# Two looped expert jobs are written out beside the four first experts of a mixture-of-experts layer

## What is computed

```python
def swiglu(x, w_gu, w_down, width):
    h = x @ w_gu
    return (jax.nn.silu(h[..., :width]) * h[..., width:]) @ w_down

def moe_swiglu(x, w_router, w_gu, w_down):
    logits = jnp.einsum('btd,de->bte', x, w_router)
    top_val, top_idx = lax.top_k(logits, TOP_K)          # TOP_K = 2
    gate = ...                                           # softmax of the two, zero elsewhere
    out = jnp.zeros_like(x)
    for e in range(N_EXPERTS):                           # 8
        out = out + gate[..., e:e + 1] * swiglu(x, w_gu[e], w_down[e], D_EXPERT)   # 3584
    return out
```

## Time and profile before

| | |
|---|---|
| median of three runs | 1716.98 us |
| the profiled execution, and its span | 1711.11 us, 1709.4 us |
| mean granted clock of TensorE | 0.972 |
| first-jobs stage (743.6 to 1198.8): TensorE, VectorE, ScalarE busy | 401.6, 127.9, 107.8 us of 455.2 |
| the same: share of the DMA engines, rate | 1.03, 400 GB/s |
| a looped job (1322.1 to 1441.0): TensorE, VectorE, ScalarE busy | 118.9, 104.6, 88.5 us of 118.9 |
| the same: share of the DMA engines, rate | 1.00, 379 GB/s |

### The profile page before, as it was taken

How to read it: one execution, slowest core, us unless ns; L and a number is a source line. 1 busy time by engine, 2 the same in 40 slices (tenths; PEclk the granted TensorE clock), 3 DMA queues, 4 the chain that set the end, 5 groups by cost and what they waited for, 6 DMA issues and landing times.

```text
span 1709.4 us, 27459 instructions
## 1 busy us (share of the span) xinstructions
PE 1598.7 (94%) x10674; PEld 1213.7 (71%) x10674; DVE 998.5 (58%) x1233; ACT 750.8 (44%) x829; POOL 139.5 (8%) x247
## 2 busy tenths in 40 slices
PE   8999999999988999999899989786899999999897
PEld 6768999998866666854445535454688888888685
DVE  4668655456645554672223212231788888888797
ACT  4225543335343223252213212221677777777575
POOL 1231000000032450020000000000000000000300
PEclk9999999999999999999999999898999999999998
DMA  9969554444142350059999999999999999999992
GB/s 240 255 163 304 140 166 142 139 136 137 59 139 61 114 159 9 2 221 409 403 395 404 406 404 400 404 402 397 410 401 369 397 376 360 403 356 384 388 361 108
DMA packets 232252, 466.83 MB, mean 273 GB/s; under 512 B 25205, under 2 KB 121620, under 8 KB 232129
## 3 DMA queue, kind: packets, MB, share of 16 engines
q1 hardware_dynamic: 217246, 426.81, 68.7%
q0 software_dynamic: 11744, 31.62, 6.1%
q10 hardware_dynamic: 3155, 6.93, 1.2%
HBM read 445.78 MB, written 19.99 MB: 272 GB/s over the span
## 4 chain that ended last, share of the span: by engine, by line
PE 76%; DMA 8%; DVE 6%; ACT 4%; issue 3%; POOL 1%; ACTq 0%; SPq 0%; POOLq 0%; DVEq 0%
PE ps L2726 10%; PE ps L2882 8%; PE ps L2883 8%; PE ps L2884 8%; PE ps L2163 6%; PE ps L2165 6%; PE ps L2164 6%; DMA raw<-in_moe_w_gu 4%; PE ps L2719 3%; PE ps L2720 2%; PE ps L2721 2%; PE ps L2568 2%; DMA raw<-in_moe_w_down 2%; PE ps L2531 2%; PE ps L2607 2%
## 5 line engine op out<-in xcount | busy, mean ns | idle before, releaser
L2014 DVE TENSOR_TENSOR w_lo<-raw,w_hi 128x2048 fp32r<-128x2048 f32 x168 | 383.2, 2291 | 62.2 <-ACT w_hi L1302 61.0
L1302 ACT ACTIVATE w_hi<-raw 128x2048 fp32r<-128x2048 f32 x168 | 322.3, 1919 | 133.6 <-PE ps L2884 116.0
L2020 DVE TENSOR_TENSOR w_lo<-raw,w_hi 128x2048 fp32r<-128x2048 f32 x42 | 96.3, 2292 | 229.1 <-ACT w_hi L1309 228.2
L2163 PE MATMUL ps<-x_hi,w_hi 128*128 128x304 f32 x656 | 202.8, 309 | 2.8 <-DVE x_lo L1566 1.7
L2165 PE MATMUL ps<-x_lo,w_hi 128*128 128x304 f32 x656 | 198.0, 302 | 0.0
L2164 PE MATMUL ps<-x_hi,w_lo 128*128 128x304 f32 x656 | 197.1, 300 | 0.0
L2882 PE MATMUL ps<-w_hi,g_hi 128*128 128x512 f32 x448 | 177.9, 397 | 12.3 <-DVE w_lo L2014 12.1
L2883 PE MATMUL ps<-w_lo,g_hi 128*128 128x512 f32 x448 | 176.2, 393 | 0.0
L2884 PE MATMUL ps<-w_hi,g_lo 128*128 128x512 f32 x448 | 176.2, 393 | 0.0
L1437 DVE TENSOR_TENSOR w_lo<-raw,w_hi 128x2048 fp32r<-128x2048 f32 (+4 forms) x129 | 135.5, 1095 | 67.8 <-ACT w_hi L1044 67.6
L2726 PE MATMUL ps<-raw,g_s 128*32 128x128 f32 (+3 forms) x1920 | 161.3, 377 | 10.3 <-DMA raw<-in_moe_w_gu 10.3
(11 more groups left out here) (472 smaller groups left out, 2506.0 us busy)
## 6 DMA issues: line engine op xcount, KB each, us to landing
raw<-in_moe_w_gu SPq DMA_DIRECT2D x224, 1024.0 KB, 9.9
raw<-in_moe_w_down SPq DMA_DIRECT2D x112, 1024.0 KB, 9.0
raw<-in_ffn_w_gu SPq DMA_DIRECT2D x44, 512.0 KB, 5.2
raw<-in_conv_w_in SPq DMA_DIRECT2D x16, 512.0 KB, 8.4
raw<-in_ffn_w_down SPq DMA_DIRECT2D x16, 512.0 KB, 4.5
kvn<-in_cache_ckv POOLq DMA_DIRECT2D x64, 128.0 KB, 3.5
kvn<-in_cache_ckv SPq DMA_DIRECT2D x64, 128.0 KB, 2.7
rows_in<-zrow POOLq DMA_DIRECT2D x13, 512.0 KB, 10.4
```

The lines of the kernel that those rows point to most:

```text
L1302: nc.scalar.activation(w_hi[:, u % SPLIT], raw[:, u % RAW], ACT.Copy).then_inc(hi_done, 1)
L2014: V.tensor_tensor(w_lo[:, u % SPLIT], raw[:, u % RAW], w_hi[:, u % SPLIT].bitcast(F32), ALU.subtract).then_inc(lo_done, 1)
L2020: V.tensor_tensor(w_lo[:, n % F_SPLIT], first_raw(k), w_hi[:, n % F_SPLIT].bitcast(F32), ALU.subtract).then_inc(lo_done, 1)
L2163: nc.tensor.matmul(out, hi, xh, start=start, stop=False, skip_group_check=True)
```

## The change

The first two jobs of the loop, called E and F, move into the written-out stage, so that six jobs, 252 units, are run there and two are left in the loop. E and F run as H does, in seven half-width steps, without extra rows. H, E and F make one stream, C, A and B (in that order) the other, and a unit of one alternates with a unit of the other. The streams have PSUM banks of their own: gates and ups of the wide one in 0 and 2, the narrow one's in 3 and 6 (C in 3 alone), H's extra rows in 1 and their output in 6. A turn still follows on its step's last unit, except that a wide job's last turn comes after one narrow unit.

H's extra rows now come after the main product instead of before it. The buffers of E and F come free when the unit is split. The token rows of E, F and the first looped job are fetched to `xrow` 12 units into the wide job before, or early in the list, and turned in banks 0 and 2 between the two last down units of the wide job before. The 128-row outputs of H and E are copied and stored by ScalarE (`early_out`) right behind their last units; F's is stored as H's was, in the first looped job. The job table's count is lowered by two, and waits in the loop count from there.

```diff
-SMALL_AFTER = (2, 2, 1, 2, 2, 1, 2)
+EARLY_JOBS = 2
+STATIC = FIRST_JOBS + EARLY_JOBS
+SMALL_ORDER = "CAB"
+BIG = "HEF"
+BIG_STEPS = 2 * STEPS - 1
+def big_units():
+    seq = []
+    for i, x in enumerate(BIG):
+        for s in range(BIG_STEPS):
+            seq += [[("gate", x, s, part)] for part in range(2)]
+            if s:
+                seq += [[("down", x, s - 1, part)] for part in range(2)]
+            seq += [[("up", x, s, part)] for part in range(2)]
+            if s < BIG_STEPS - 1:
+                seq[-1].append(("turn", x, s, 0))
+        seq += [[("down", x, BIG_STEPS - 1, 0), ("rows", x, i, 0)], [("down", x, BIG_STEPS - 1, 1)]]
+    return seq
+def small_units():
+    seq, before = [], None
+    for x in SMALL_ORDER:
+        for s in range(STEPS):
+            n = 2 * wide(x, s)
+            gates = [[("gate", x, s, part)] for part in range(n)]
+            downs = [[("down",) + before + (part,)] for part in range(2 * wide(*before))] if before else []
+            while gates or downs:
+                seq += gates[:2] + downs[:2]
+                gates, downs = gates[2:], downs[2:]
+            seq += [[("up", x, s, part)] for part in range(n)]
+            seq[-1].append(("turn", x, s, 0))
+            before = (x, s)
+    return seq + [[("down",) + before + (part,)] for part in range(2 * wide(*before))]
 def first_jobs_schedule():
+    big, small, seq = big_units(), small_units(), []
+    for n, group in enumerate(big):
+        kind, x, s, part = group[0]
+        closes = kind == "up" and s == BIG_STEPS - 1 and part == 1
+        seq += group
+        follow = 0 if n in (0, 2, len(big) - 1) else 2 if closes else 1
+        for q in range(follow):
+            if closes and q == 1:
+                seq.append(("turn", x, s, 0))
+            seq += small.pop(0)
...
+X_UP = SLOTS
+SMALL_AT = {(x, kind): (3, 256 if kind == "up" else 0) if TILES[x] == 4 or kind == "gate" else (6, 0) for x in SMALL for kind in ("gate", "up", "turn")}
+X_OUT = 6
...
     def wait_place_free(engine, k):
         q = last_in_place(k)
-        engine.wait_ge(unit_used, U_MOE + (0 if q is None else q + 1))
+        if q is not None and FIRST_UNITS[q][1] in BIG[1:]:
+            engine.wait_ge(lo_done, U_MOE + SPLIT_NO[q] + 1)
+        else:
+            engine.wait_ge(unit_used, U_MOE + (0 if q is None else q + 1))
...
+            if x in BIG[1:] and k == FIRST_OF[x]:
+                sp.wait_ge(table_ready, 1)
+                i = BIG.index(x) - 1
+                e = sp.value_load(jobi[0:1, i:i + 1], min_val=0, max_val=NEXP - 1)
+                gates[x], downs[x] = gate_src(e), down_src(e)
...
+            if x in BIG[1:] and k == FIRST_OF[x] + 12:
+                i = BIG.index(x)
+                sp.wait_ge(m_g, i)
+                sp.dma_start(xrow[:], rows_in[PLACES + i * SLOTS:PLACES + i * SLOTS + SLOTS]).then_inc(rows_ld, 16)
...
+        def early_out(i, e):
+            act.wait_ge(unit_used, U_MOE + e + 1)
+            act.wait_ge(y_st, 16 * i + 16)
+            nc.scalar.activation(y_row[:], ps[:, 4:6, :].rearrange("p b n -> p (b n)"), ACT.Copy).then_inc(m_yc, 1)
+            act.wait_ge(m_yc, i + 1)
+            act.dma_start(rows_out[PLACES + SLOTS * i:PLACES + SLOTS * i + SLOTS], y_row[:]).then_inc(y_st, 16)
...
+            if kind == "gate" and part == 0 and s == 0 and x in BIG[1:]:
+                pe.wait_ge(m_gl, BIG.index(x))
+            if kind == "up" and part == 0 and TURNED_BEFORE[k]:
+                pe.wait_ge(f_tl if x in BIG else f_ts, TURNED_BEFORE[k])
+            if kind == "gate" and part == 0 and x in SMALL and TURNED_BEFORE[k]:
+                pe.wait_ge(f_ts, TURNED_BEFORE[k])
+            if kind == "up" and part == 0 and x in SMALL:
+                pe.wait_ge(f_sp, SMALL_N[x, s] + 1)
```

More of the change, by code:

```diff
@@ L110 @@
 HALF = SLOTS // 2
-SMALL_AFTER = (2, 2, 1, 2, 2, 1, 2)
 FIRST_JOBS = 4
+EARLY_JOBS = 2
+STATIC = FIRST_JOBS + EARLY_JOBS
 SMALL = "ABC"
+SMALL_ORDER = "CAB"
+BIG = "HEF"
+BIG_STEPS = 2 * STEPS - 1
 def wide(x, s):
-    return 1 if x == "H" else HALVES[s]
-def first_jobs_schedule():
[L122 to L148, removed]
@@ L149, in first_jobs_schedule @@
+def first_jobs_schedule():
+    big, small, seq = big_units(), small_units(), []
[8 more added lines that the diff above has]
+            seq += small.pop(0)
+    assert not small
     return seq
@@ L725, in wait_place_free, with row_banks, rows_of, split_slot @@
         q = last_in_place(k)
-        engine.wait_ge(unit_used, U_MOE + (0 if q is None else q + 1))
+        if q is not None and FIRST_UNITS[q][1] in BIG[1:]:
+            engine.wait_ge(lo_done, U_MOE + SPLIT_NO[q] + 1)
+        else:
+            engine.wait_ge(unit_used, U_MOE + (0 if q is None else q + 1))
+    def row_banks(bank, step):
+        return ps[:, bank:bank + step + 1:step, :]
+    def rows_of(g):
+        return g[:].rearrange("p (b c) s -> p b (c s)", b=2)
+    def split_slot(k):
+        return (SPLIT_NO[k] + 1) % F_SPLIT
+    def small_rows(x, kind, s):
+        bank, at = SMALL_AT[x, kind]
+        return ps[:, bank, at:at + narrow(x, s)]
     def narrow(x, s):
@@ L868, in _ @@
                 wait_place_free(sp, k)
-            fetch_unit(first_raw(k), downs[x](s, part, x == "H") if kind == "down" else gates[x](kind, s, part, x == "H"), first_ready(k))
+            if x in BIG[1:] and k == FIRST_OF[x]:
[3 more added lines that the diff above has]
+                gates[x], downs[x] = gate_src(e), down_src(e)
+            fetch_unit(first_raw(k), downs[x](s, part, x in BIG) if kind == "down" else gates[x](kind, s, part, x in BIG), first_ready(k))
             if k == RAW + 4:
@@ L2821, in small_unit @@
                     c = (4 // n) * part + q
-                    m = plain_tiles(x, 0 if kind == "gate" else 2, narrow(x, s), token_rows(x, c), w, 512 * n * q, c == 0, c == DC - 1)
+                    if kind == "gate" and s == 0 and x == SMALL_ORDER[0]:
+                        pe.wait_ge(f_gl, c + 1)
+                    bank, at = SMALL_AT[x, kind]
+                    m = plain_tiles(x, bank, narrow(x, s), token_rows(x, c), w, 512 * n * q, c == 0, c == DC - 1, to=at)
             return m
```

225 lines of the change are left out of this document (123 added, 102 removed).

## The result

The changed kernel takes 1727.19 us (median of five runs, 1725.4 to 1730.91) against 1716.98: ratio 1.0059, 95% interval 1.0037 to 1.0082. It is 10 us slower where 6.6 us less was forecast. The profiled execution took 1727.35 us around a span of 1725.7; that of before lay 6 us under its median.

A forecast was written before the change was run, and what follows sets the result against it. The prediction held the first-jobs stage bound by transfers and looped jobs by TensorE. It summed 677.8 + 2 + 2 - 2 = 679.8 against 686.4 us, 6.6 saved: 1717.0 - 6.6 = 1710 us, range 1695 to 1735.

The forecast's parts named there:

- The sum's terms for the transfers: Merged stage: 2.72 us per 2 KB unit, 2.564 per 4 KB unit; transfers need 677.8 us, 8.6 less than 686.4.
- TensorE's price of a pair: Merged stage: alternating wide and narrow units cost 2.95 + 1.87 us; TensorE needs 659 us, 97% of the transfers' 677.8.
- rival (a): Merged stage: TensorE becomes the bound through waits at turns; 1759 us, or 1724 with half the waits; chance 0.22.
- Rival (c): Stage transfers: H's own work, not 2 KB rows, lowers the rate; 1702 us, or 1698 without end losses; chance 0.14.
- The loop at full clock: Loop's start: the first ten matmuls take 0.23 us instead of 0.43, 2.0 us less.
- The lag at the start: Stage's start: TensorE stands 9 to 11 us behind landings; transfers lose 2 us, between 0 and 8.
- rival (b): Start and turns: lag takes 3 to 8 us more transfer time, no measurable change; 1713 to 1718 us, chance 0.22.
- Eight buffers are 8 x 2.65 = 21 us ... so up to 14 us of lag costs nothing: Stage's buffers: 7 of 21 us keep transfers in flight, so TensorE may lag landings by up to 14 us free.
- After a turn the next narrow gate needs the copy that stands behind the split ... hidden: After turns: ScalarE's copy comes at landing + 2.6 us, TensorE is due about 5 us behind landing; no cost.
- If that cover goes, 2 to 3 us at each of three ends: Output copies and row split: 6.7 us of units cover about 4 needed; without cover, 2 to 3 us per end.
- Six of H, twelve of E and F ... 39.0: Stage's turns on TensorE: 10.2 + 15.6 + 9.6 + 3.6 = 39.0 us, with waits for VectorE's product as in the rows.
- The wait of SP for TensorE should shrink: Sign in the merged stage: SP's transfer queue waits less for TensorE while landing times stay above 7 us.

The follow-up runs named there:

- e4: e1 with gates and ups of H, E and F read in 4 KB rows instead of 2 KB (wrong columns, same bytes): 1710.50 us, ratio 0.9957.
- e6: e5 without the third product (tokens' lower, weights' upper part) in the stage's wide units: 1712.37 us, ratio 0.9974.
- e1: Changed kernel with the stage's eight buffers visited in the order 4, 5, 0, 1, 2, 3, 6, 7: 1718.72 us, ratio 1.0023.
- e3: e1 with the turns of E and F one narrow unit later: 1718.08 us, ratio 1.0003.
- e11: e10 with VectorE's products for the wide steps also ahead of the split: 1710.21 us, ratio 0.9963.
- e5: e3 with ScalarE's copies of turns and turned token rows ahead of the split three units ahead: 1711.99 us, ratio 0.9960.
- e12: e10 with the changed kernel's buffer order put back: 1715.82 us, ratio 0.9993.
- e2: Kernel before with the buffer order of e1, which there puts the hand-over defect in: 1722.59 us, ratio 1.0030.
- e10: e5 with VectorE's product for a narrow step right behind its last up unit, ahead of the split: 1707.38 us, ratio 0.9942.
- e9: Kernel before with ScalarE's copy of a turn ahead of the split three units ahead: 1718.55 us, ratio 0.9998.

## Why the prediction was wrong

**What held.** The sum's terms for the transfers: 397 to 401 GB/s with the 2 KB units among them, 2.72 us for such a unit (2.705 by e4). TensorE's price of a pair (4.82, 4.86 measured), and that it fits below the transfers: in the middle its 95% load costs no transfer time, and e6 with 116 us less of it is no faster. So rival (a) gives about the right time, 1724 and up, by a mechanism that the middle of the stage does not show. Rival (c) fell with e4: a 2 KB row does lower the rate. The Trainium skill (DMA: Bandwidth & Descriptors, Why small descriptors are slow) has the direction right; the estimate of 0.06 us a unit from it is under half of the 0.135 between e1 and e4. The loop at full clock gave back 4 us, where 2 were taken. The lag at the start was bounded by 0 and 8 us, and the traces show nearly all of that range: from 780 to 840 nothing is lacking in e3, e6 and e11, 5.1 us in the changed kernel and 7.4 in e5, where the clock had been low during the gathers. A start like that of e5 takes back what the change gains, as rival (b) had it.

**What failed, first of all: "Eight buffers are 8 x 2.65 = 21 us ... so up to 14 us of lag costs nothing".** The step took the number of buffers for the distance between two uses of one. At the end of the stage that distance is two units, because the count of units, 252, meets the change from eight to six in another phase than 168 did. Price: 6 us by e1 (1.0059 - 1.0023), 8.8 by e12 (0.9993 - 0.9942), each known to about 5 us; e2 makes a loss of 5 us in the kernel before. This alone takes about the forecast gain away. The prediction weighs when a buffer comes free, and nowhere which buffer each of the last units gets.

**Second: "After a turn the next narrow gate needs the copy that stands behind the split ... hidden", and the same for the output copies.** It was weighed for a pair in the middle of a job, where it holds. At H's end the last turn, the token rows of E, their split and a narrow turn all come within 13 us. The copy of the turn stands behind a split that waits for a landing, to 978.86, and that of the token rows behind one that waits for TensorE, to 987.73. TensorE frees buffers late and SyncE issues nothing from 989.83 to 997.89. Moving the copies ahead gave 0.43% (7 us, e3 to e5) and the dip of 332 GB/s became 398. "If that cover goes, 2 to 3 us at each of three ends" named this end and that of the stage, with too small a size for H's (5 us); at E's end nothing is lost (398 to 402 GB/s from 1200 to 1240).

**Third: "Six of H, twelve of E and F ... 39.0" for the turns, with VectorE's product waited for only as in the rows.** When narrow units ran four at a time, TensorE was seldom so close behind the landings that VectorE stood waiting in a split. In the new order it is, at the last turn above all: 7.77 us of idle in the changed kernel (with the late landing of the hand-over in it), 4.06 in e6, 0.52 in e10. Late turns (e3) gave 0.20%, the product ahead (e10) 0.18%, each inside its interval, together with e5 clearly outside.

The ratios of e1, e3, e5 and e10 form one chain, 6.2 + 3.4 + 7.4 + 3.1 = 20.1 us from the changed kernel to e10; that they add up is no test. The profiles are one. What the slices of 20 us lack against 401 GB/s, in us of transfers:

| | stage | start (780 to 840) | H's end (980 to 1020) | last (1400 to 1460) | stage less the three |
|---|---|---|---|---|---|
| changed | 702.8 | 5.1 | 4.6 | 15.3 | 677.8 |
| e1 | 696.2 | 6.0 | 5.1 | 6.8 | 678.3 |
| e3 | 689.3 | 0.2 | 5.2 | 5.6 | 678.3 |
| e5 | 690.5 | 7.4 | 0.1 | 3.7 | 679.2 |
| e10 | 681.9 | 2.2 | 0.1 | 2.2 | 677.4 |
| e12 | 692.4 | 5.5 | 0 | 9.4 | 677.5 |

Without the three places every one of these stages takes 677 to 679 us, where the sum had 677.8 for the transfers. So the loss lies in them whole. Places (e1, e12) move the last column, ScalarE's copies (e5) the third and some of the last, VectorE's product (e10) goes with 1.5 us of the last, and the start varies by itself: e3's stage is shorter than e1's almost only by its start, so the late turns show no gain of their own. With 2 us lost at the start and 2 at the end, as the sum had it, e10's stage is the 681.8 forecast, and with 4 us instead of 2 won in the loop its median is 1707.4 against 1710. The mechanism of the gain was right; waits that the sum had at nothing cost the changed kernel some 18 us more than e10, and its start 3 more.

"The wait of SP for TensorE should shrink" failed too. In the stage before it was 277 us (62% of it), in the changed one 522 (74%), in e10 406 (60%). What the queue waited for (us in total, times, longest us) in the changed kernel is:

```profile
SPq L907 <- PE ps L2798: 522.0, 162, 13.7
```

TensorE frees the buffers late all through, at a lag that the buffers still cover in the middle (rate 400). The wait by itself is no measure of what is lost: before has 62% of it at full rate.

**Open.** The stage begins between 753 and 766 us from profile to profile, of kernels before and after alike (before 755.6, e9 762.6, e12 753.5, e10 765.9); that is work ahead of the change, and much of the scatter of one kernel's times may come from it. Why the granted clock differs during the gathers (0.69 to 1.00 from 760 to 780) was not settled, nor whether it is what makes the loss at 780: 0.69 and 0.71 go with 315 and 300 GB/s there, 1.00 with 402 and more, but 0.83 with 319 in e12 and 402 in e6. No run changed the start alone.

## What to carry to other kernels

When units are added to a written-out sequence over a ring of buffers, list for the last and first units which unit held the buffer before: a change of the number of buffers was harmless at 168 units and cost 6 to 9 us at 252. Where an engine does its work in order, look for what another engine waits for behind a step that waits for a transfer. The places to check are the ends of jobs: in the steady middle, and in the kernel before (e9), the same order cost nothing that could be measured. A sum over steady rates tells what is to be had; the loss sits in the few stretches of 20 us that a table of windows shows at once.

## What was not expected of the hardware

TensorE's clock and its waits fed each other at the ends: after 7.77 us of idle a narrow unit took 3.68 us instead of 1.94, at a granted clock of 0.50, and after 4.06 us (e6) and 3.23 us (e3) of idle the same, while in e10, with 0.52 us of idle, the unit behind the turn took 1.94 at a granted clock of 1.00. At these places a wait of 3 to 8 us cost the wait and nearly two more. And the rate of 401 GB/s did not move when TensorE's busy time went from 337 us (e5) to 281 (e6) of 360: there its work and the transfers did not disturb each other.
